# A weight ring in SBUF: slots 2 and 3 start at 448 past a multiple of 512 bytes, slots 0 and 1 at 128

## What is computed

```python
x = x + mla_mixer(rms_norm(x, g), ...)            # first block, layer 0
x = x + sqrelu_mlp(rms_norm(x, g), w1, w2)        # relu(x @ w1)^2 @ w2, 1024 -> 4096 -> 1024
x = x + mlstm_mixer(rms_norm(x, g), ...)          # layer 1, and again sqrelu_mlp
h = h + 0.5 * swiglu_ffn(rmsnorm(h, g), w_in, w_out)   # four times, 1024 -> 2 x 2816 -> 1024
h = h + short_conv_mixer(rmsnorm(h, g), ...)      # second block, layer 0
h = h + nsa_mixer(rmsnorm(h, g), ...)             # layer 1
```

## Time and profile before

| | |
|---|---|
| median of 3 runs | 1565.78 us (1564.8 to 1567.98) |
| the profiled execution | 1565.57 us |
| its span in the trace | 1563.8 us, mean granted clock 0.999 |
| PE busy | 1551.1 us, 99% |
| VectorE busy | 1042.3 us, 67% |
| ScalarE busy | 849.8 us, 54% |
| mean DMA rate | 180 GB/s |

### The profile page before, as it was taken

The page is one execution under the profiler, slowest core; times in us unless marked ns, Lnnn a source line. Parts: engine busy times, 40 slices in busy tenths (PEclk is TensorE's granted clock), DMA queues, the critical chain, the costliest instruction groups (busy, mean ns, idle before and its releaser), DMA issues.

```text
span 1563.8 us, 35291 instructions
## 1 busy us (share of the span) xinstructions
PE 1551.1 (99%) x12910; PEld 1511.7 (97%) x12910; DVE 1042.3 (67%) x1751; ACT 849.8 (54%) x1301; POOL 123.9 (8%) x123
## 2 busy tenths in 40 slices
PE   9999999999999999999999999999999999999999
PEld 8899999988999999999999999989999988999999
DVE  7677765643876557666787766678576656676664
ACT  6776654545655445555445555556555546655542
POOL 1830000036000000000000000000000032200000
PEclk9999999999999999999999999999999999999999
DMA  7246666554555565566565666656566971065654
GB/s 242 69 129 193 191 188 202 169 169 148 181 195 189 191 201 185 191 194 198 188 208 192 192 192 195 202 180 206 187 192 196 226 208 55 15 201 190 195 195 148
DMA packets 80784, 281.02 MB, mean 180 GB/s; under 512 B 8880, under 2 KB 12464, under 8 KB 80688
## 3 DMA queue, kind: packets, MB, share of 16 engines
q1 hardware_dynamic: 76800, 274.78, 54.8%
q10 hardware_dynamic: 3888, 4.85, 1.6%
HBM read 278.03 MB, written 1.57 MB: 179 GB/s over the span
## 4 chain that ended last, share of the span: by engine, by line
PE 95%; DVE 3%; ACT 1%; issue 0%; DMA 0%; SPq 0%; ACTq 0%; DVEq 0%
PE psum L1731 27%; PE psum L1732 27%; PE psum L1735 27%; PE psum L1860 2%; PE psum L1862 2%; PE psum L1861 2%; PE psum L2149 1%; PE psum L2100 1%; PE psum L2133 1%; PE psum L2047 0%; DVE w_lo L1018 0%; PE psum L1924 0%; PE psum L1724 0%; PE psum L1914 0%; PE psum L2094 0%
## 5 line engine op out<-in xcount | busy, mean ns | idle before, releaser
L551 ACT ACTIVATE w_hi<-raw 128x1024 fp32r<-128x1024 f32 x518 | 547.1, 1058 | 488.8 <-PE psum L1735 441.5
L1018 DVE TENSOR_TENSOR w_lo<-raw,w_hi 128x1024 fp32r<-128x1024 f32 x484 | 592.0, 1223 | 255.4 <-ACT w_hi L551 254.8
L1731 PE MATMUL psum<-xs,w_hi 128*128 128x256 f32 x1928 | 536.3, 278 | 1.7 <-DVE w_lo L1018 1.6
L1735 PE MATMUL psum<-xs,w_lo 128*128 128x256 f32 x1928 | 533.5, 277 | 0.0
L1732 PE MATMUL psum<-xs,w_hi 128*128 128x256 f32 x1928 | 533.0, 276 | 0.0
L1731 PEld LDWEIGHTS psum<-xs,w_hi 128*128 128x128 f32 x1928 | 362.0, 188 | 2.7 <-DVE w_lo L1018 2.1
L1732 PEld LDWEIGHTS psum<-xs,w_hi 128*128 128x128 f32 x1928 | 361.9, 188 | 0.3
L1735 PEld LDWEIGHTS psum<-xs,w_lo 128*128 128x128 f32 x1928 | 362.0, 188 | 0.0
L1731 PE MATMUL psum<-hs,w_hi 128*128 128x256 f32 x1280 | 354.6, 277 | 0.0
L1735 PE MATMUL psum<-hs,w_lo 128*128 128x256 f32 x1280 | 354.0, 277 | 0.0
L1732 PE MATMUL psum<-hs,w_hi 128*128 128x256 f32 x1280 | 353.5, 276 | 0.0
(11 more groups left out here) (284 smaller groups left out, 1485.2 us busy)
## 6 DMA issues: line engine op xcount, KB each, us to landing
raw<-tiles SPq DMA_DIRECT2D x518, 512.0 KB, 4.2
bias<-bias_dram ACTq DMA_DIRECT2D x8, 256.0 KB, 7.7
x<-x_in SPq DMA_DIRECT2D x4, 256.0 KB, 5.1
w1c_all<-w1c_k ACTq DMA_DIRECT2D x4, 256.0 KB, 4.8
w1c_all<-w1c_v ACTq DMA_DIRECT2D x4, 256.0 KB, 6.2
y_out<-x SPq DMA_DIRECT2D x8, 128.0 KB, 3.4
con<-consts SPq DMA_DIRECT2D x1, 771.0 KB, 8.8
bias_dram<-bias_row ACTq DMA_DIRECT2D x1, 512.0 KB, 7.1
```

The source lines that it names most:

```text
L551: act.activation(w_hi[s][:, :], raw[s][:, :], ACT.Copy).then_inc(hi_ready, 1)
L1018: dve.tensor_tensor(w_lo[s][:, :], raw[s][:, :], hi_of(w_hi[s][:, :]), ALU.subtract).then_inc(lo_ready, 1)
L1731: pe.matmul(out, w_hi[s][:, c:c + P], x_hi, start=first, stop=False)
L1735: return pe.matmul(out, w_lo[s][:, c:c + P], x_hi, start=False, stop=last)
```

## The change

The high and low buffers of a slot now stand beside each other: w_hi0, w_lo0, w_hi1, w_lo1, then 320 bytes which nothing uses (`apart_w`), then w_hi2, w_lo2, w_hi3, w_lo3. So the weights of slots 2 and 3 start at 448 past a multiple of 512. raw stays where it is. Everything from `x` to `vc` moves up by 320 bytes, and `apart` becomes 320 bytes shorter, so that `os`, `xs`, `hs` and `bias` stay where they were. No instruction, wait or transfer is added or taken away.

```diff
-        w_hi = [sb(f"w_hi{s}", [P, TILE], F32R) for s in range(RING)]
-        w_lo = [sb(f"w_lo{s}", [P, TILE], F32R) for s in range(RING)]
+        w_hi, w_lo = [], []
+        for s in range(RING):
+            if s == RING // 2:
+                sb("apart_w", [P, 80])
+            w_hi.append(sb(f"w_hi{s}", [P, TILE], F32R))
+            w_lo.append(sb(f"w_lo{s}", [P, TILE], F32R))
         x = sb("x", [P, KD * S])
...
-        sb("apart", [P, 120])
+        sb("apart", [P, 40])
         with nc.sbuf_tensor("os", [P, KD * 2 * S], F32R) as os_:
```

## The result

| | before | after |
|---|---|---|
| median | 1565.29 us (4 runs, 1564.33 to 1567.98) | 1595.34 us (4 runs, 1594.48 to 1595.5) |
| ratio to before | | 1.019, 95% interval 1.0177 to 1.0203 |
| span of the profiled execution | 1563.8 us | 1593.4 us |

The change costs 30 us. Slower was forecast, at 1586 us.

A forecast was written before the change was run, and what follows sets the result against it. PE's matmul pace was taken to bound the kernel. The profiled 1565.57 us plus 19.8 for slots 2 and 3 in fast stretches, other terms nothing, gave 1585.4, as a median 1586 us; range 1556 to 1612.

The forecast's parts named there:

- What bounds the kernel: Whole kernel: PE, busy 99% of the span, is limited only by its matmul pace, not waits, other engines or clock.
- Distance 0 in slots 2 and 3, fast stretches: 4,600 matmuls of 256 columns, forecast to go from 113.3 to 117.6 ns each, 19.8 us lost; chance 0.36.
- upper bound of 13.2 ns: Products of slots 2 and 3: worst extra time per 256-column matmul, argued from 512-column products; upper end 69 us.
- Slow stretches: 950 matmuls of slots 2 and 3 at the slow pace: between 4.1 us gained and nothing; taken as nothing.
- The 512-column products: Token-major products, 243 of them at distance 0: between -6.6 and +6.6 ns each, 1.6 us either way; taken as nothing.
- DVE and ACT passes, the small tensors: Passes over the slots at new addresses, small tensors moved 320 bytes: some 0.4 us more per pass would stay hidden.
- Reading of the odd matmuls: Feed-forward stages: pace 117.6 ns until the third small matmul of line 1724, 113.3 after it.
- address does not matter: Rival for all products: only timing, shifted by the odd matmul, sets the pace; time stays 1565.8 us; chance 0.15.
- The rule of the Trainium skill: PE's reads of SBUF: two independent ports, PE never waits, so no change, 1565.8 us; given less weight.
- Fast pace lost for all slots: Rival: slots 2 and 3 shift the timing and the fast pace isn't found again; 39.6 us, 1605; chance 0.16.
- Full clash: Rival in slots 2 and 3: both reads in the same place from their start; up to 1635 us; 0.10 including intermediate cases.
- Chances: Odds of measurable outcomes: slower 0.62, same 0.15, faster 0.23; slow preferred because the fast pace hardly ever comes by itself.

## Why the prediction was right, and where it was off

- **What bounds the kernel.** Right: waits, other engines and the clock play no part after the change either.
- **Distance 0 in slots 2 and 3, fast stretches.** The pattern was right (two tiles fast, two tiles slower, in turn), the reason and the size were not. I took these matmuls for ones whose timing doesn't fit, at the slow pace of before: +4.3 ns and 19.8 us. Measured are +6.6 ns and 29.8 us. The slow pace is one of two timings at distance 320, while 0 has one pace of its own, 120.0, as the kernel with all slots at 448 shows. The upper bound of 13.2 ns held it.
- **Slow stretches.** I took nothing, with a gain of up to 4.1 us as the bound. Nothing is what they gave, but by luck, as the sum of two terms that I did not have: slots 2 and 3 cost 120.0 there (1.9 us lost), and they set the timing so that slots 0 and 1 become fast in some of these stretches (1.9 us gained).
- **The 512-column products.** Between -1.6 and +1.6 us; -1.1 us is what they gave. Distance 0 is better for them (226.7 ns against 233).
- **DVE and ACT passes, the small tensors.** Hidden, as said: 1224 and 1058 ns, PE's waits for w_lo at 2.4 us. The mean durations of the products rose to 280 and 281 ns, not to 278 as forecast.
- **Reading of the odd matmuls.** I read every feed-forward stage as slow until the third of them. It is not so. In glu_0, cin and glu_1 the first two tiles run at 113.3 ns, as these two rows of before in glu_0 show, 36 matmuls apart:

```profile
583.99 0.28 PE L1731 MATMUL psum<-xs,w_hi 128*128 128x256 f32 x1
...
588.07 0.28 PE L1731 MATMUL psum<-xs,w_hi 128*128 128x256 f32 x1
```

The second halves of the MLPs begin at 113.3 too, until the first odd matmul makes them slow (117.8); the third makes them fast again. The sum does not use this reading, but it hid that small matmuls also lead from fast to slow.
- **The rivals.** That the place alone counts is out (both moved: no change), and so is "address does not matter". The rule of the Trainium skill ("SBUF - State Buffer", "Who interferes with whom"), by which PE has two independent read ports and never waits on anyone, does not fit these runs: the distance between its two reads alone makes 1629.8 us out of 1566.2. "Fast pace lost for all slots" is out: slots 0 and 1 stay at 113.3. "Full clash" was nearest in kind, at half the price of its bound.
- **Chances.** My reason for slow rather than fast was that the fast timing hardly ever comes by itself. That was true of distance 320, and said little about 0: at 448, another distance, four of the seven stages up, glu and cin settle at the fast pace without any odd matmul. It gave the right sign for a reason that holds only in part.

## What to carry to other kernels

- Where PE is busy all the time with short matmuls that each load new weights, count the matmuls in a window before looking for anything else; a pace with two values in one program is worth 4% of such a stage. Then look at where stationary and moving operand start, modulo 256 and 512 bytes, and move one of them alone.
- A filler matmul or a spacer that was fitted by trial holds for one layout. Fitted to distance 320, the three odd matmuls made distance 448 slow, so a change of layout and the fillers have to be tried together.

## What the hardware showed that was not expected

- A product of 256 columns of fp32r with a load of 128 columns costs 113.3, 117.8 or 120.0 ns at the full clock, by the distance of the two reads: 120.0 at 0 and 256, 113.3 or 117.8 at 192, 320 and 448, 117.8 at 64 (113.3 not seen), irregular between 116 and 120 at 128, 288, 352, 384 and 480. The 512-column form with the roles exchanged costs 226.7 at 0 and 233 at 192.
- At distances 320 and 448 the pace has a memory. It lasts over 1,500 matmuls, and a matmul of 60 columns can shift it, and so can the sums of a norm. At 320, in the kernel before, these sums left the slow pace in all six stages; at 448 they turned one pace into the other in all 18 places. A tile of 24 matmuls at distance 0 left the tiles at 320 right behind it fast, with one exception in some 300 places; one matmul in twelve did not.
- What state in the chip keeps that timing, and why 120.0 sets it, stays open. A collision in the memory where both reads take place is my reading of it, and was only argued.
